# Seven up-projection units of an MLP as seven half-size block products

## What is computed

```python
h2 = rms_norm(x, norm_mlp[layer])
x = x + jnp.square(jax.nn.relu(h2 @ w_ff1[layer])) @ w_ff2[layer]
```

## Time and profile before

| | us |
|---|---|
| median of 3 runs | 1691.41 (1690.8 to 1692.02) |
| profiled execution | 1689.05 |
| its span, in which all times of the trace lie | 1687.4 |
| PE busy | 1672.0 (99%) |
| DVE busy | 896.4 (53%) |
| ACT busy | 618.6 (37%) |
| granted TensorE clock, mean | 0.999 of full speed |

### The profile page before, as it was taken

How to read it: one execution, slowest core, us unless ns; L and a number is a source line. 1 busy time by engine, 2 the same in 40 slices (tenths; PEclk the granted TensorE clock), 3 DMA queues, 4 the chain that set the end, 5 groups by cost and what they waited for, 6 DMA issues and landing times.

```text
span 1687.4 us, 23046 instructions
## 1 busy us (share of the span) xinstructions
PE 1672.0 (99%) x9378; PEld 1217.1 (72%) x9378; DVE 896.4 (53%) x1217; ACT 618.6 (37%) x744; POOL 112.8 (7%) x168
## 2 busy tenths in 40 slices
PE   9999999999999999999999999999999999999998
PEld 7888888865454535454588877788888888888886
DVE  6425438452343334324668755567675544773487
ACT  6334433321111101111366633344642245652565
POOL 4000000000000000000011012210000001100100
PEclk9999999999999999999999999999999999999999
DMA  7332222948999999999541332124352358756974
GB/s 274 100 99 75 75 75 101 354 189 342 429 428 428 428 429 429 428 429 428 204 153 53 100 100 75 51 76 132 107 188 100 107 181 195 157 149 221 200 157 128
DMA packets 90703, 353.29 MB, mean 209 GB/s; under 512 B 7856, under 2 KB 7872, under 8 KB 78208
## 3 DMA queue, kind: packets, MB, share of 16 engines
q1 hardware_dynamic: 78288, 325.95, 50.4%
q0 software_dynamic: 12336, 26.23, 7.8%
HBM read 345.87 MB, written 6.29 MB: 209 GB/s over the span
## 4 chain that ended last, share of the span: by engine, by line
PE 97%; DMA 1%; DVE 1%; ACT 0%; issue 0%; POOL 0%; DVEq 0%; POOLq 0%; ACTq 0%
PE bank L2764 51%; PE bank L3117 12%; PE bank L3522 9%; PE bank L3130 7%; PE bank L3025 4%; PE bank L3065 3%; PE bank L3297 2%; PE bank L2789 2%; PE bank L2810 1%; DMA ring<-in_w 1%; PE bank L3327 1%; PE bank L3350 1%; PE bank L3397 1%; PE bank L3222 1%; PE bank L3430 0%; PE bank L3436 0%
## 5 line engine op out<-in xcount | busy, mean ns | idle before, releaser
L2764 PE MATMUL bank<-act_hi,w_hi 128*128 128x512 f32 x992 | 390.0, 393 | 0.0
L2764 PE MATMUL bank<-act_hi,w_lo 128*128 128x512 f32 x992 | 386.2, 389 | 0.0
L2764 PE MATMUL bank<-act_lo,w_hi 128*128 128x512 f32 x992 | 386.2, 389 | 0.0
L1754 DVE TENSOR_TENSOR w_lo<-w_stage,w_hi 128x2048 fp32r<-128x2048 f32 x79 | 181.1, 2293 | 208.9 <-ACT w_hi L1044 208.8
L1044 ACT ACTIVATE w_hi<-w_stage 128x2048 fp32r<-128x2048 f32 x79 | 151.4, 1917 | 242.0 <-PE bank L2764 223.7
L3117 PE MATMUL bank<-ring,xgT 128*64 128x512 f32 x992 | 216.1, 592 | 1.8 <-ACT xgT L1266 1.4
L2764 PEld LDWEIGHTS bank<-act_hi,w_hi 128*128 128x128 f32 x992 | 186.2, 188 | 40.8 <-issue 2.9
L2764 PEld LDWEIGHTS bank<-act_hi,w_lo 128*128 128x128 f32 x992 | 186.2, 188 | 39.1
L2764 PEld LDWEIGHTS bank<-act_lo,w_hi 128*128 128x128 f32 x992 | 186.3, 188 | 37.7
L3117 PEld LDWEIGHTS bank<-ring,xgT 128*64 128x64 f32 x992 | 71.0, 137 | 143.0 <-issue 139.5
L3130 PE MATMUL bank<-ring,gatedT 128*64 128x512 f32 x512 | 113.4, 595 | 3.1 <-DMA ring<-in_w 2.3
(11 more groups left out here) (490 smaller groups left out, 2366.6 us busy)
## 6 DMA issues: line engine op xcount, KB each, us to landing
ring<-in_w SPq DMA_DIRECT2D x94, 2048.0 KB, 16.8
w_stage<-in_w_in SPq DMA_DIRECT2D x42, 1024.0 KB, 5.1
w_stage<-in_w_ff SPq DMA_DIRECT2D x24, 1024.0 KB, 5.6
b_sum<-in_w_ff POOLq DMA_DIRECT2D x12, 1024.0 KB, 12.7
w_stage<-in_w_out SPq DMA_DIRECT2D x8, 1024.0 KB, 5.0
b_one<-in_w_ff SPq DMA_DIRECT2D x6, 1024.0 KB, 7.7
branch_gates<-gate_out POOLq DMA_DIRECT2D x16, 256.0 KB, 2.5
w_stage<-in_w_proj_gla SPq DMA_DIRECT2D x4, 1024.0 KB, 9.9
```

What stands on the lines that cost most here:

```text
L1754: dve.tensor_tensor(w_lo[s][:, 0:ktiles, :], w_stage[s][:, 0:ktiles, :], w_hi[s][:, 0:ktiles, :].bitcast(F32), ALU.subtract).then_inc(w_lo ...
L2764: ins = pe.matmul(banks[j][:, :], left, right, start=(kc == 0 and k == 0 and n_pass == 0), stop=(kc == g.chunks - 1 and k == g.ktiles - 1 ...
```

## The change

Unit 0 stays as it was. Units 1 to 7 become seven block products each (products 0 to 6), written (u, n) below. A product multiplies a 256-column by 512-row weight block, or a sum of such blocks, with a 512-row by 256-token block of the transposed activations, or a sum: 24 pairs with 256 moving columns.

- Activations: ACT copies the transposed `h2` whole into `raw_T`; DVE makes four sums T1 to T4 once (`t_add`), split into `t_hi` and `t_lo`. In the second half T2 to T4 are split again, since the down product has overwritten them.
- Weights: per unit DVE makes four sums W1 to W4 (`w_add`) and splits seven operands (`slot_low`, with ACT's `slot_high`) into three slots that are used in turn. All are 128x1024 elements. A third stage buffer is added; `STAGE_ORDER` deals the blocks to the three.
- Outputs: ACT copies three banks (`copy_first`, `copy_both`, `copy_fifth`), DVE adds a bank to each (`blk_add`: 11, 22, 12), and ACT does three relus on the sums, one from PSUM (`relu_last`), and four squares.
- Down: the split weights lie in other buffers (`down_hi`, `down_lo`); the work is the same. The first split of a half (`part_split_hi(h, 0)`, `part_split_lo(h, 0)`) waits for products of the last unit, since it overwrites T2 and T3. The negations of `b_sum` stand at the end of units 1, 2 and of 4, 5; those of `b_one[1]` and `b_far` at the end of units 3 and 6. POOL's adds to `b_sum[0]` both come ahead of those to `b_sum[1]`.

The core of the diff (the product counts, a product on PE, the end of a half on ACT, SP's loads around the first half):

```diff
-    for _ in range(HALVES):
-        up = Gemm(last, FH // 512, 2, "act")
-        last = Gemm(up, 2, PARTS, "dve", tiles=PARTS)
+    g_up = Gemm(g_out2, 1, 2, "act")
+    for h in range(HALVES):
+        g_blk.append(Gemm(g_down[-1] if h else g_up, HALF_UNITS if h else HALF_UNITS - 1, PARTS, "act", tiles=3))
+        g_down.append(Gemm(g_blk[h], 2, PARTS, "dve", tiles=PARTS))
...
+            def block_product(u, n):
+                pe.wait_ge(w_lo_done, blk_split(u, n))
+                elif n == 2:
+                    pe.wait_ge(out_act, blk_copied(u, CP_FIRST))
+                    pe.wait_ge(n_lo, T_LOWS + (5 if half_of_unit(u) else 1))
+                elif n == 4:
+                    pe.wait_ge(out_act, blk_copied(u, CP_BOTH))
+                elif n == 6:
+                    pe.wait_ge(n_lo, T_LOWS + (7 if half_of_unit(u) else 4))
+                    pe.wait_ge(out_dve, blk_added(u, ADD_22))
+                for f in range(2):
+                    cols = slice(f * P, (f + 1) * P)
+                    for k in range(4):
+                        for n_pass, (left, right) in enumerate(((hi, b_hi), (hi, b_lo), (lo, b_hi))):
+                            ins = pe.matmul(bank[:, 256 * f:256 * f + 256], left[:, k, cols], right[:, k, :],
...
                 step_split_hi(h, 1)
+                relu_sum(units[-1], ADD_12, blk_both)
+                square(units[-1], 0, 1, blk_both)
+                relu_last(units[-1])
+                square(units[-1], 1, 0, blk_last)
                 part_split_hi(h, 1)
...
+            third_made(2)
+            load_blocks(3, 1)
+            unit_split(2)
+            load_step(0, 0)
+            third_made(3)
+            load_step(0, 1)
+            for kc in range(2):
+                sp.wait_ge(w_lo_done, step(0, kc))
+                load_step(0, 2 + kc)
```

More of the change, by code:

```diff
@@ new lines, in blocks, with blk_copied, blk_added @@
+        def blocks(u):
+            near, far = (stage[stage_in((u, k))[0]] for k in range(2))
+            return near[:, :, 0:256], far[:, :, 0:256], near[:, :, 256:512], far[:, :, 256:512]
+        CP_FIRST, CP_BOTH, CP_FIFTH = 1, 2, 3
+        ADD_11, ADD_22, ADD_12 = 1, 2, 3
+        def blk_copied(u, n):
+            h = half_of_unit(u)
+            return g_blk[h].tile0 + 4 + 3 * (u - units_of(h)[0]) + n
+        def blk_added(u, n):
+            h = half_of_unit(u)
+            return sums_added[h] + 4 + 3 * (u - units_of(h)[0]) + n
@@ new lines, in _ @@
+            load_step(1, 1)
+            for kc in range(2):
+                sp.wait_ge(w_lo_done, step(1, kc))
+                load_step(1, 2 + kc)
+            sp.wait_ge(part_low, V_PARTS + PARTS + 3)
+            sp.wait_ge(hid_summed, summed_in(1) + S4)
+            sp.dma_start(b_one[0][:, :, :], weight_block(1, 1, 1, 0)).then_inc(b_one_in[0], 16)
+            sp.wait_ge(w_lo_done, step(1, 8))
+            sp.dma_start(b_one[1][:, :, :], weight_block(1, 1, 1, 1)).then_inc(b_one_in[1], 16)
@@ L3525, in part_passes @@
                 ins.then_inc(pe_tiles, 2)
[L3527 to L3531 removed]
+            first_up(g_up)
+            for h in range(HALVES):
+                for u in units_of(h):
+                    for n in range(PARTS):
+                        block_product(u, n)
                 for n in range(PARTS):
```

527 lines of the change are left out of this document (391 added, 136 removed).

## The result

The changed kernel takes 1693.13 us (median of 20 runs), the kernel before 1690.82 in the same comparison: a ratio of 1.0017, 95% interval 1.0010 to 1.0024. The forecast was 1689.8, 1.6 us less than the 1691.41 of the three runs that it started from. The changed kernel is 2.3 us slower instead: a small loss, but clear of the noise.

What follows compares the result with a forecast made beforehand. PE, 99% busy, was taken to bound the kernel: gain 11.2 + 0.2 us less waits of 9.8 gives 1.6, so 1691.41 - 1.6 = 1689.8 us (chance 0.53), range 1685.5 to 1693.5.

Steps and rivals of the forecast that it cites:

- The gain of the pairs: Units 1 to 7 on PE: 21.76 us per unit falls to 20.16, a gain of 11.2 us in all.
- the sum of the waits: PE's new waits at the list ends and first-half step loads: 9.8 us in all.
- What bounds, and the pair: Whole kernel: PE bounds it, 99% busy; a pair of 256 columns takes 120.0 ns, a unit 20.16 us.
- The restart at each product: Rival: each of 49 products pays a 0.19 us restart, 9.3 us in all, time 1699; chance 0.06.
- the load not hidden: Rival: weight load not overlapped, a pair costs 218 ns, units 116 us more, about 1805; chance 0.01.
- the cheaper pairs: Rival: pairs at half of 226.7 ns, a unit 19.04 us, gain 19.0, time 1683; chance 0.02.
- Entry, unit 1: PE waits 1.2 us for ACT's list at product (1, 2) and 0.2 at product 4, sum 1.4.
- Unit 0's second weight: Entry: copies to raw_T delay this weight to 1365.3; PE wants it at 1365.36, so no wait.
- End of units 3 and 7: Product 6 waits for add 22 behind part_lo0: 1.3 us in each half, 0.3 more in unit 7, sum 2.9.
- Steps 1 and 2: First down half: ACT's and DVE's lists make PE wait 0.8 and 1.3 us; second half 0 and 0.1.
- Loads of steps 2 and 3: First down half: POOL's adds slow these loads; PE waits 3.3 us, bounds 0 to 4.1; second half 0.
- waits half as long again: Rival: handovers at the four exposed places run longer, 13 us of waits, time 1693.0; chance 0.12.

Runs made afterwards that it cites:

- x2: Changed kernel with DVE's ADD_22 ahead of the first activation block's low part in units 3 and 7: 1692.05 us, ratio 1.0007 to the kernel before.
- x13: Changed kernel with POOL's adding transfers of the first half cut to a sixteenth of their columns, waits and order kept: 1686.66 us, ratio 0.9970.
- x3: Changed kernel with unit 5's first block load issued after step 12 of the first down half instead of at step 7: 1691.26 us, ratio 1.0003.
- x10: Changed kernel, first half: both b_sum negated in unit 1, b_one[1] and b_far in unit 2, POOL's b_sum adds in turns: 1691.64 us, ratio 1.0006.
- x14: Changed kernel with x2, x3, last two norm squares ahead of unit 0's relus, first half's negations and so adds begun earlier: 1687.13 us, ratio 0.9969.
- x16: x14 with POOL's first add to b_sum[1] held until the second to b_sum[0] has landed, first half: 1687.21 us, ratio 0.9983.
- x7c: Changed kernel with x2, x3, x10 and the last two norm squares behind copy_first and slot 3 of unit 1: 1691.02 us, ratio 1.0000.
- x12: Changed kernel with x2, x3 and the first half's adds to b_one[1] and b_far behind those for steps 6 and 7: 1693.04 us, ratio 1.0006.

## Why the prediction failed, step by step

The gain of the pairs came. What failed is the sum of the waits: 9.8 us were forecast; the gain of 11.4 and the 0.3 by which the MLP is longer make it 11.7, and the late starts with their refills sum to 11.5. The largest term that was put at nothing is the reload at step 11, 1.3 us. A second one is the clock, put at nothing as well; its price in the usual run, about 1.5 us, is argued and not shown. The steps in order:

*What bounds, and the pair.* Right. 120.0 ns per pair; without the wait at (7, 6), units 4 to 7 take 81.15 us (x2), against 4 x 20.16 = 80.64. The restart at each product, the load not hidden and the cheaper pairs did not come. The rows were right to go by: the Trainium skill (TensorE: Matmul & The Clock Gate, section Back-to-back issue gap) has a formula, meant for a matmul by itself, that gives 109 ns for 256 columns, and by the timeline above a pair takes 120.

*Entry, unit 1.* Forecast 1.4. The row at 1384.60 is 0.96 late, the one at 1390.64 0.22: 1.2, with the pairs behind them 1.3. Right in place and cause.

*Unit 0's second weight, "hidden, just".* Wrong by 0.2: the row at 1366.88 starts 0.07 late and the next pairs pay a refill.

*End of units 3 and 7.* Forecast 1.3 and 1.6, measured 1.37 and 1.56 by the starts, and x2 removed both: shown.

*Steps 1 and 2.* Forecast 0.8 and 1.3, waited 0.40 and 1.08. The second down half was to lose 0.1 at its step 2 and lost 0.39, most of it there: the row at 1617.60 is 0.24 late, and a refill of 0.1 follows. Right in place; in cause as far as the lists of ACT and DVE are what was waited for.

*Loads of steps 2 and 3.* Forecast 3.3, spread over both with 1.4 at most for step 3's own; measured nothing beyond the list at step 2, 3.0 with a refill of 0.3 at step 3. The sum was right, the split wrong. Step 2's load was not slowed by the adds at all: issued at 1440.24, ahead of both, it landed in 5.1 us. Step 3's was issued 3.5 us behind the second add and had it beside it for 10 us. It landed within the bound of 12.1, and since a wait at step 2 would have put off step 3 as well, it alone sets the sum. That the adds are the cause is shown by x13.

*The end of the first down half: not in the sum.* The prediction stopped at step 3 and took the load orders behind it as harmless. The change issues two block loads of units 4 and 5 at step 7, ahead of the reload of `b_one[1]`; step 11 waited 1.0 and 0.3 of refill. x3, without the block load, and x13, with the adds cut, each removed it: shown. By parts: the units gained 6.8 where 7.1 was forecast, the first down half lost 6.7 instead of 5.4, the second 0.4 instead of 0.1. So the -1.6 of the forecast became the +0.3 that the two profiles show from unit 1 on.

*The clock: not in the sum either.* A wait of 3 us was priced at 3 us. In x2 and x3 a wait of 3.6 and 4.1 us at the same step was followed by a stretch at 1.2 GHz, which costs 1.5 more (x10), and the usual run of the changed kernel has a mean clock 0.001 under that of before. +0.3, 0.2 for unit 0 and 1.5 give 2.0 of the measured 2.3. That the usual run's fall lies at step 3 is argued, from x2, x3 and from its absence in the runs of x13; no profile of the unedited kernel caught it.

The rival that gave the right time, "waits half as long again" at 1693.0, had another mechanism: the handovers. Those held, so its time is luck. The direction of the forecast was wrong because it was a small difference of two terms of 11 and 10 us, and in the second two places were missing.

## What to carry to other kernels

When work on the bound engine shrinks, look at each transfer that was timed by its old length, through to the end of the stage and not only at the place that is edited: here the second half, with slack in its queues, gained 4.4 us, and the first half, with its adds and loads packed into a shorter time, lost 4.6. Moving such a transfer mostly moves the wait; what helped (x14, x16, each of several edits) was to begin it in time that nothing else used, and to ask of each instruction moved which queue waits for its semaphore. Both also hold the edits of x2 and x3; x7c and x12 hold these as well and took 1691.0 and 1693.0, so those two alone don't give the gain. And a short wait on TensorE can cost more than its length.
